# Twelve experts of sixteen placed by their row counts in a two-layer decoder step: 11 groups of 128 rows in each layer, their weights fetched by rank

## The reference

```python
def hier_moe(x, w_group, b_group, w_router, b_router, w1, w3, w2):
    xt = x.reshape(-1, shp[-1])
    lg = (xt @ w_group + b_group)
    g = jnp.argmax(lg, axis=-1)                       # one of 4 groups
    p_g = softmax(lg)[g]
    le_g = (xt @ w_router + b_router) restricted to group g (4 experts)
    vals, idx = lax.top_k(le_g, 2)                    # two experts of that group
    wk = softmax(vals) * p_g
    h = silu(xt @ w1[e]) * (xt @ w3[e])               # 1024 -> 256, for e in the two experts
    y = sum over the two experts of wk * (h @ w2[e])  # 256 -> 1024
```

```
layer 0: 60 60 71 33 43 62 58 73 69 58 85 104 81 56 56 71
layer 1: 72 62 74 42 55 43 100 40 6 12 9 9 114 154 160 88
```

## Time and profile before

| | |
|---|---|
| median of three runs | 1420.35 us |
| profiled launch, its own time | 1417.93 us |
| its span, first to last instruction | 1416.1 us |
| PE busy, mean granted clock | 1171.0 us (83%), 0.909 |
| expert groups, layer 0 and layer 1 | 13 and 14 |
| w1/w3 transfers of 2 MB, w2 transfers of 1 MB | 38 and 38 |

### The profile page before, as it was taken

The page is one execution under the profiler, slowest core; times in us unless marked ns, Lnnn a source line. Parts: engine busy times, 40 slices in busy tenths (PEclk is TensorE's granted clock), DMA queues, the critical chain, the costliest instruction groups (busy, mean ns, idle before and its releaser), DMA issues. The chain is left out here.

```text
span 1416.1 us, 22910 instructions
## 1 busy us (share of the span) xinstructions
PE 1171.0 (83%) x9270; PEld 705.1 (50%) x9270; DVE 400.7 (28%) x1039; ACT 266.7 (19%) x699; POOL 56.5 (4%) x76
## 2 busy tenths in 40 slices
PE   7899999879975999927987988788867971999970
PEld 5688888745452333226875765444543430333320
DVE  2133332244430111144011223332333333111117
ACT  2122222030111111142110132122242010111114
POOL 4000000000011000020000000000000002000002
PEclk9999999979987999968999899899869995999995
DMA  9953332188156999975979963999552524699955
GB/s 339 382 177 93 99 98 70 64 306 328 50 218 238 365 423 424 307 251 194 342 282 346 350 214 118 351 367 358 211 203 111 245 119 168 258 412 425 425 206 191
DMA packets 134728, 358.53 MB, mean 253 GB/s; under 512 B 10319, under 2 KB 67840, under 8 KB 123486
## 3 DMA queue, kind: packets, MB, share of 16 engines
q1 hardware_dynamic: 117358, 293.79, 56.7%
q0 software_dynamic: 9344, 34.92, 6.3%
q10 hardware_dynamic: 7920, 28.35, 5.1%
HBM read 309.69 MB, written 47.33 MB: 252 GB/s over the span
## 5 line engine op out<-in xcount | busy, mean ns | idle before, releaser
L1294 PE MATMUL bank<-W,XT 128*32 128x512 f32 x1728 | 195.2, 604 | 2.4 <-DVE XT L1369 2.4
L1294 PEld LDWEIGHTS bank<-W,XT 128*32 128x32 f32 x1728 | 53.9, 111 | 124.2 <-issue 120.6
L1058 PE MATMUL bank<-WOUT,CAT 128*128 128x512 f32 x256 | 111.6, 594 | 0.0
L2028 PE MATMUL bank<-XT,W 128*128 128x260 f32 x448 | 109.8, 400 | 0.7 <-ACT Q L2177 0.4
L471 PE MATMUL bank<-XT,WH 128*128 128x260 f32 x448 | 100.0, 384 | 0.0
L1316 PE MATMUL bank<-WD,GT 128*32 128x512 f32 x864 | 98.2, 595 | 1.5 <-DVE GT L1390 1.5
L2028 PEld LDWEIGHTS bank<-XT,W 128*128 128x128 f32 x448 | 86.2, 198 | 21.7 <-issue 8.0
L471 PEld LDWEIGHTS bank<-XT,WH 128*128 128x128 f32 x448 | 84.6, 190 | 13.3
L471 PE MATMUL bank<-WH,XT 128*128 128x256 f32 x384 | 84.0, 379 | 0.0
L471 PEld LDWEIGHTS bank<-WH,XT 128*128 128x128 f32 x384 | 72.5, 190 | 10.0 <-issue 0.4
L1058 PEld LDWEIGHTS bank<-WOUT,CAT 128*128 128x128 f32 x256 | 48.0, 190 | 57.9 <-issue 57.8
(11 more groups left out here) (390 smaller groups left out, 1286.6 us busy)
## 6 DMA issues: line engine op xcount, KB each, us to landing
W<-in_w13f SPq DMA_DIRECT2D x38, 2048.0 KB, 15.7
PGS<-in_KP SPq DMA_DIRECT2D x128, 384.0 KB, 5.2
PGS<-in_VP SPq DMA_DIRECT2D x128, 384.0 KB, 5.2
WD<-in_w2f SPq DMA_DIRECT2D x38, 1024.0 KB, 16.0
CAT<-XS ACTq DMA_DIRECT2D x27, 512.0 KB, 9.2
WH<-in_w_a SPq DMA_DIRECT2D x13, 1024.0 KB, 11.9
XS<-CAT POOLq DMA_DIRECT2D x20, 512.0 KB, 16.0
WOUT<-in_w_out SPq DMA_DIRECT2D x4, 2048.0 KB, 12.6
```

The source lines that it names most:

```text
L1058: last = nc.tensor.matmul(PB[2 * (i % 2) + c][:, :], CAT[:, k, t * P:(t + 1) * P], w_out(c)[:, k, :], start=(k == 0), stop=(k == KC - 1))
L1294: last = nc.tensor.matmul(PB[2 + g % 2][32 * j:32 * j + 32, :], XGT[:, g % 2, k, 32 * j:32 * j + 32], W13[:, LANES[g][j] % WRING, k, :], s ...
L2028: last = nc.tensor.matmul(PB[u["bank"]][0:u["m"], 0:u["w"]], u["lhsT"](w, k), u["rhs"](w, k), start=(k == 0), stop=(k == KC - 1))
```

## The change

Experts 0 to 3 keep their three chunks each. The other twelve are sorted on the chip by their number of rows, largest first (ties by the lower number), and each gets the place of its rank. A place has a fixed position in the sequence and a fixed number of chunks:

- layer 0: ranks 0 to 11 have 4, 3, 3, 3, 3, 3, 3, 2, 2, 2, 2, 2 chunks, in that order
- layer 1: the places stand in the order rank 0 (5 chunks), 8 (1), 1 (5), 9 (1), 2 (4), 10 (1), 3 (4), 11 (1), 4 (3), 6 (2), 5 (3), 7 (2)

Both add up to 44 chunks with the first four experts, so 11 groups in each layer. The sure extra tiles are gone; an overflowing expert's rows go to the loop of `extra_tiles`. Only four experts' weights are loaded ahead of the routing. From entry 4 on, SP reads the expert's number of that rank from a new table `EXP`, which DVE writes after the slots, and it starts on that once the first group's rows have landed. DVE computes the rank of each expert by comparing all twelve counts with each other (144 elements in a row), and from it each expert's first row and capacity.

```diff
+RANKS = ([(r, 4 if r == 0 else 3 if r < 7 else 2) for r in range(NR)],
+         [(0, 5), (8, 1), (1, 5), (9, 1), (2, 4), (10, 1), (3, 4), (11, 1), (4, 3), (6, 2), (5, 3), (7, 2)])
+CHUNKS = [[CAP // CH] * FIXED + [c for r, c in RANKS[l]] for l in range(2)]
+NG = sum(CHUNKS[0]) * CH // P
...
-                        for e in (0, 3, 4):
+                        for e in (0, 3):
                             load_w13(sp, l, e, e)
-                        for e in range(WRING):
+                        for e in range(FIXED):
                             load_w2(sp, l, e, e)
...
+                    nc.tensor.matmul(PB[4][:, 0:NE], const("ones"), OTH[:, NT, :], start=True, stop=True).then_inc(rk_ready, 1)
                     nc.tensor.matmul(PB[3][:, 0:NT * NE], const("before"), MS[:, 2, :, :].rearrange("p t e -> p (t e)"),
                                      start=True, stop=False)
...
+                    link(stt(KEY[:, 0, :], count[:, FIXED:NE], float(NE), const("iotaov")[:, FIXED:NE], ALU.mult, ALU.subtract))
+                    link(tt(SORT[:, 0, :, :], KEY[:, 0, :].unsqueeze(1).broadcast_to(square), KEY[:, 0, :].unsqueeze(2).broadcast_to(square), ALU.is_gt))
+                    link(red(KEY[:, 1, :], SORT[:, 0, :, :], AX.X, ALU.add))
...
             def on_sp(sp):
-                of = [e if e is not None else sp.value_load(EL[0:1, i - NE:i - NE + 1], min_val=0, max_val=NE - 1)
-                      for i, e in enumerate(SEQUENCE[l])]
-                for i in range(WRING, len(of) + 1):
-                    if i < len(of):
-                        sp.wait_ge(h_done, LAST[i - WRING] + BG + 1)
+                def expert_at(i):
+                    rank = RANKS[l][i - FIXED][0]
+                    return sp.value_load(R["EXP"][0:1, rank:rank + 1], min_val=0, max_val=NE - 1)
+
+                of = {}
+                sp.wait_ge(xg_in[0], 16 * (1 + xg_before[0]))
+                for i in range(FIXED, NE + 1):
+                    if i < NE:
+                        of[i] = expert_at(i)
+                        if i >= WRING:
+                            sp.wait_ge(h_done, LAST[l][i - WRING] + BG + 1)
                         load_w13(sp, l, i, of[i])
-                    if i > WRING:
-                        sp.wait_ge(y_done, LAST[i - 1 - WRING] + BG + 1)
+                    if i > FIXED:
+                        if i - 1 >= WRING:
+                            sp.wait_ge(y_done, LAST[l][i - 1 - WRING] + BG + 1)
                         load_w2(sp, l, i - 1, of[i - 1])
```

More of the change, by code:

```diff
@@ L46 @@
 OVER = 16
-SURE = (2, 4)
-NG12 = NE * CAP // P
-ROWS = NE * CAP + OVER * OVR
+CH = 32
+FIXED = 4
+NR = NE - FIXED
+RANKS = ([(r, 4 if r == 0 else 3 if r < 7 else 2) for r in range(NR)],
+         [(0, 5), (8, 1), (1, 5), (9, 1), (2, 4), (10, 1), (3, 4), (11, 1), (4, 3), (6, 2), (5, 3), (7, 2)])
+CHUNKS = [[CAP // CH] * FIXED + [c for r, c in RANKS[l]] for l in range(2)]
+NG = sum(CHUNKS[0]) * CH // P
+assert all(sum(c) * CH == NG * P for c in CHUNKS)
+ROWS0 = NG * P
+ROWS = ROWS0 + OVER * OVR
 WRING = 5
@@ L88, in _constants @@
     add("iota4", np.tile(np.arange(4)[None, :], (P, NT)))
-    add("slotbase", np.tile(CAP * np.arange(NE)[None, :], (P, 1)))
-    add("ovbase", np.tile(CAP * np.arange(NE)[None, :] + CAP - NE * CAP, (P, 1)))
-    add("past", np.tile(CAP + OVR * np.arange(7)[None, :], (P, 1)))
+    add("past", np.tile(OVR * np.arange(7)[None, :], (P, 1)))
+    places = np.zeros((2, 2, NE))
+    for l in range(2):
+        begin = CH * (np.cumsum(CHUNKS[l]) - CHUNKS[l])
+        for i, chunks in enumerate(CHUNKS[l]):
+            at = i if i < FIXED else FIXED + RANKS[l][i - FIXED][0]
+            places[l, :, at] = begin[i], CH * chunks
+    add("places", np.tile(places.reshape(1, -1), (P, 1)))
     add("iotaov", np.tile(np.arange(OVER)[None, :], (P, 1)))
@@ L992, in build @@
         GA = xt_flat[:, 2 * D + 512:3 * D].rearrange("p (u n) -> p u n", u=2)
[L994 to L998, removed]
+        LANES, LAST = [], []
+        for l in range(2):
+            of_chunk = [i for i, c in enumerate(CHUNKS[l]) for _ in range(c)]
+            LANES.append([of_chunk[4 * g:4 * g + 4] for g in range(NG)])
+            LAST.append([max(g for g in range(NG) if i in LANES[l][g]) for i in range(NE)])
         def expert_landed(i, l):
-            return 16 * (i // WRING + 1 + l * len(range(i % WRING, len(SEQUENCE[0]), WRING)))
+            return 16 * (i // WRING + 1 + l * len(range(i % WRING, NE, WRING)))
         def load_w13(eng, l, i, e):
@@ L1114, in route @@
         def route(l, R):
[L1118 to L1119 removed]
+            LG, GH, T4, LEG, HK, MS, OTH, RK, SW2, SLU, WT2, OV, OVF, ELF, EL, SORT, OH, KEY, BC, EXP = (
+                R[n] for n in ("LG", "GH", "T4", "LEG", "HK", "MS", "OTH", "RK", "SW2", "SLU", "WT2", "OV", "OVF", "ELF", "EL",
+                               "SORT", "OH", "KEY", "BC", "EXP"))
+            places = const("places").rearrange("p (l q e) -> p l q e", l=2, q=2)[:, l]
             bias = SMALL[:, 16 + 20 * l:36 + 20 * l]
@@ L1146, in _ @@
                     nc.tensor.matmul(PB[3][:, 0:NT * NE], const("ones"), OTH[:, 0:NT, :].rearrange("p t e -> p (t e)"),
-                                     start=False, stop=True)
-                    nc.tensor.matmul(PB[4][:, 0:NE], const("ones"), OTH[:, NT, :], start=True, stop=True).then_inc(rk_ready, 1)
+                                     start=False, stop=True).then_inc(rk_ready, 1)
                     if l == 0:
@@ L1289, in hidden @@
                         pe.wait_ge(g_ready, g + BG - 1)
-                    for i in sorted(set(LANES[g]) - set(LANES[g - 1] if g else [])):
+                    for i in sorted(set(LANES[l][g]) - set(LANES[l][g - 1] if g else [])):
                         pe.wait_ge(w13_in[i % WRING], expert_landed(i, l))
```

65 lines of the change are left out of this document (40 added, 25 removed).

## The result

| | before | after |
|---|---|---|
| median of 4 runs each on one chip, us | 1419.53 (1411.63 to 1420.96) | 1375.6 (1370.02 to 1379.58) |
| ratio, 95% interval | | 0.9711 [0.9674, 0.9748] |
| profiled execution, us | 1417.93 | 1370.02 |
| its span, us | 1416.1 | 1368.2 |
| groups, w1/w3 transfers | 27, 38 | 22, 32 |

The change takes 2.9% off, 43.9 us. The forecast was 1368, with a range of 1361 to 1379. The profiled execution, 1370.02 us, is the fastest of the four.

The account below looks back on a forecast made before the run. TensorE was taken as the bound, 11.966 us a group, with DMA also full. 1417.93 - 59.83 (groups) + 4.65 (routing) + 2.3 (wait) + 1 (border) = 1366.05 us; named 1368, as the timed median lay 2.4 us higher; range 1361 to 1379.

Parts of the forecast that it names:

- the forecast's own 1363 to 1373: Whole kernel: TensorE still the bound with one short wait, 1363 to 1373 us, chance 0.66.
- rivals 1 and 2: Rival 1: weights become the bound, 1378 us, chance 0.14; rival 2: layer border gives part back, 1377 us, chance 0.10.
- The groups: Expert stage, both layers: 27 groups become 22, each missing one a TensorE period of 11.966 us, 59.83 us saved.
- The routing: DVE, before the slots: nine linked instructions added, less a matmul wait; 4.65 us added over both layers, bounds 4.5 and 7.7.
- The weights in layer 1: Layer 1, ahead of group 9: bunched w1/w3 transfers make TensorE wait once, 2.3 us, bounds 0 and 8.7.
- Layer 0: Layer 0's weights: the tight transfer, w13(15) for group 10, lands with 4.4 us to spare, so no wait.
- The border: Between the layers: half slabs of layer 1's projection overlap layer 0's last two stores; 1 us added, bounds 0 and 6.7.
- The sum: Whole launch: 1417.93 - 59.83 + 4.65 + 2.3 + 1 = 1366.05 us against the profiled launch, named as 1368 for the median.
- The bytes as the bound: DMA queues in both layers: at 0.383 MB/us, 12.3 us of weight waits instead of 2.3, 1378 us, chance 0.14.
- The border (1377): Between the layers: later last stores and gathers cost 8.7 us more than counted, 1377 us, chance 0.10.
- The surplus tiles: Loop for overflowing experts: places too small, 22 to 24 us a tile, 1456 us with four tiles, chance 0.03.
- The better case: Layer 1 and the border: no wait and a free border, 1364 us, lower with a cheaper ranking, chance 0.07.

Follow-up runs that it names:

- e4_rank_twice: The changed kernel with the six ranking instructions run twice in a row in both layers: 1377.91 us, ratio 0.974 to the kernel before.
- e2_spread: The changed kernel with only layer 1's places reordered so that transfers come evenly: 1367.83 us, ratio 0.9667 to before; repeated, 1371.7 us, ratio 0.9645.
- e3_descending: The changed kernel with only layer 1's places reordered, from large to small (ranks 0 to 11 in a row): 1390.87 us, ratio 0.9822 to before.
- e7_half_weights: e2_spread's kernel with each w1/w3 transfer from entry 5 on bringing only the first half of its 2 MB: 1369.18 us, ratio 0.965 to before.
- both orders together: The changed kernel with e2_spread's layer 1 order and layer 0's 4-chunk place last: 1364.81 us, ratio 0.9613; repeated, 1367.49 us, ratio 0.9616 to before.

## Why the prediction was right, step by step

The bound, the place of the wait and its cause were right, and the gain was forecast too large: 52 us against 43.9. The median, 1375.6, lies inside the range of 1361 to 1379, but outside the forecast's own 1363 to 1373; the range holds it because it was drawn to take in rivals 1 and 2, whose 1378 and 1377 are nearer to it than 1368. The profiled launch, 1370.02 against a sum of 1366.05, looks closer than it is: its unchanged first stage happened to be 5.5 us shorter than in the profile that the sum starts from.

**The groups**, -59.83 forecast. The period held to the hundredth in both layers. Layer 0 fell by 23.25 us against 23.93 for two groups. The 0.7 us are its first product. TensorE's timeline, of before and then of after:

```profile
442.02 9.09 PE L1294 MATMUL bank<-W,XT 128*32 128x512 f32 x64 [0.78 <-DVE XT L1369]
```

```profile
438.55 9.77 PE L1336 MATMUL bank<-W,XT 128*32 128x512 f32 x64 [0.78 <-DVE XT L1411]
...
1182.55 9.82 PE L1336 MATMUL bank<-W,XT 128*32 128x512 f32 x64 [0.78 <-DVE XT L1411]
```

The windows of after around it, columns as in the earlier trace rows:

```profile
430.00:438.50 8.50, 1.97 (x8) 1.57 (x8) 0.69 (x1) 0.68 (x2) 0.00 (x0) 0.50 0.70 251
438.50:449.00 10.50, 10.45 (x71) 3.11 (x72) 0.19 (x1) 1.58 (x2) 0.00 (x0) 0.74 0.71 242
```

The first product runs while the granted clock comes back from 0.50, the 1.2 GHz level, and in both layers it became 0.6 to 0.7 us longer (1.3 us in all), which I had not reckoned. It is not simply the longer idle time before it. In before TensorE had idled 14.27 us ahead of layer 0's first turned tile, in after 16.29; but in e4_rank_twice, with 18.08 us, the product took 8.87 us (8.80 in layer 1). Why it moves was not tested.

**The routing**, +4.65 forecast, +2.33 + 2.05 = 4.38 measured up to the slots. The first products follow it almost at the old distance (-0.42 and +0.05 us). e4_rank_twice shows that further work there delays the first product, and that half of such a delay can be gone at that product's end.

**The weights in layer 1**, +2.3 forecast within 0 to 8.7, 5.96 measured. Place, transfer and cause were named: SP issues w13(13) and w13(14) in a bunch. SP's timeline in after, and from the views of line L1020 their time to landing:

```profile
1266.99 0.33 SPq L1020 DMA_DIRECT2D W<-in_w13f  x1
...
1273.26 0.33 SPq L1020 DMA_DIRECT2D W<-in_w13f  x1
```

```profile
DMA to landing us min/median/max: 19.7/19.7/19.7
```

```profile
DMA to landing us min/median/max: 21.1/21.1/21.1
```

w13(14) took 21.1 us; the working had 1312 - 1292.9 = 19.1. That 2.0 us is most of the mis-sizing of the wait itself (4.4 instead of 2.3). The windows of after over the backlog, from the issue of w2(9) to the landing:

```profile
1254.00:1294.00 40.00, 36.05 (x319) 12.32 (x318) 7.22 (x14) 5.11 (x10) 0.00 (x0) 1.00 1.01 417
```

The DMA engines were full, at 417 GB/s and not 424. By the working's own sum the 12.6 MB then need 38.3 us instead of 37.4, which is 0.9 of the 2.0 us; the other 1.1 stay open. A term was missing besides: after the wait the next product ran at a lower clock and took 1.40 us longer. In the other five profiles with this order of layer 1 the same stage was 3.7 to 5.8 us over e2_spread's 126.47 (3.7 in e4_rank_twice, where the first product was 1.0 us shorter). This is the step that was sized at less than half. With another order (e2_spread) all of it is gone from the profile. That the order decides is shown by e2_spread and e3_descending; that it does so through the bunches is read from the times of issue.

**Layer 0**: no wait, as forecast.

**The border**, +1 forecast within 0 to 6.7. The mark came 2.04 us later, the last store 7.3 us after its issue instead of 5.2. The forecast had all four half slabs start 7.4 us before the last product's end. The first two did, at 6.8 and 5.8; the other two wait for the last group that uses entry 14, which is now the last group of all, and came 0.1 and 3.6 us behind it, in the time of the last store. Whether the next stage feels it stays open: six profiles with marks from 12.2 to 17.4 arrive at the same 579.3, and the other six with the new routing, with marks from 14.4 to 24.0, scatter from 576.0 to 586.2.

**The sum.** 59.83 less 4.38, 5.96, 1.3 and 2.04 is 46.2 us. The profiles without their first stage differ by 42.4. The 3.7 us between the two are stages that the sum leaves out, above all the 2.2 us between the layers and the 2.25 us at layer 1's mark, both within the scatter. The medians of the comparison differ by 43.9. The median after lies 7.6 us over 1368: 3.7 are the wait, 1.3 the first products and 1.0 the border, less 0.3 for the routing; the remaining 1.9 us have no named cause.

**The rivals.** The bytes as the bound (1378): its number was near, 2.4 us over the median. In sum the bytes are not the bound, since the same bytes cost no wait in e2_spread and 18.1 us in e3_descending, and half of them save nothing in e7_half_weights. Full DMA engines ahead of one late transfer are what it had right, and the forecast had that too. The border (1377) did not show in six of the profiles and is open in the rest. The surplus tiles did not occur, and were priced too low: 29.7 us each, not 22 to 24, so that the gain would have been gone with the second tile. The better case (1364) is near what both orders together reach, 1364.81 and 1367.49.

## What to carry to other kernels

Where a full engine and a full queue run side by side, the mean rate says little; the order of the pieces decides. Sizes that alternate (5 chunks, 1 chunk) free several ring places with one group, the loads bunch, and the one behind the bunch is late; spread the small pieces, and do not leave them to the end, where the same bytes cost 17.7 us more here. Count a wait at the rate of that moment, and add the slower matmuls behind it. Extra serial work in a routing step that everything waits for delays the first group by nearly its length, so it must be set against what it saves: here 4.4 us for 59.8. And hold a difference of a few us in one stage against the scatter of that stage in the same kernel before giving it a cause.

## What the runs showed of the hardware that was not expected

- A wait of TensorE of 3.93 us for data was followed by a product of 8.47 us instead of 7.07 at a mean granted clock of 0.87; 0.50 us of wait was followed by none of it (7.07). In five other profiles waits of 2.70 to 3.92 us were followed by products of 8.65 to 8.77 us, and one of 12.12 us by 8.94.
- The unchanged first stage of the program took 318.4 to 318.7 us in three profiled executions and 323.8 to 326.6 in the eleven others. A difference of 5.5 us between two single profiles can thus be no effect of the edit.
